# Dilated attention moved into the middle run's block, and the final output moved into the second run with its first two rows of tokens split early

## The reference, cut to what matters

```
first_block:  h = rms_norm(x)
              a = gelu/silu branch with a spatial mix of tokens
              b = attention over 12 heads in three groups, dilated by 1, 4 and 16,
                  joined by the groups' maxima and sums of exponentials
              m = attention over 256 memory tokens
              x = x + (gates_0 * (a @ proj_a) + gates_1 * (b @ proj_b) + gates_2 * (m @ proj_m)) @ w_out
second_block: h = rms_norm(x) * (1 + scale) + shift
              y = [ssm branch | differential attention, 4 heads | window attention]
              x = x + gate * (y @ w_out_2)
              return rms_norm(x, final_gain)
```

## Time and profile before

| | us |
|---|---|
| median of 3 runs | 1859.37 (1856.37 to 1862.62) |
| the profiled execution, its own time | 1859.85 |
| its span | 1858.1 |
| PE busy | 1764.0 (95%) |
| DVE busy | 914.3 (49%) |
| ACT busy | 654.6 (35%) |
| POOL busy | 248.9 (13%) |

### The profile page before, as it was taken

One profiled execution on the slowest core, in us unless ns is written; L12 is line 12 of the kernel. 1 busy time (PEld: TensorE's weight loads), 2 busy tenths in 40 slices (PEclk: granted clock), 3 DMA queues, 4 the chain that ended last, 5 costly groups with the idle time before them and its releaser, 6 DMA issues. The chain is left out here.

```text
span 1858.1 us, 22280 instructions
## 1 busy us (share of the span) xinstructions
PE 1764.0 (95%) x8828; PEld 1430.4 (77%) x8828; DVE 914.3 (49%) x1504; ACT 654.6 (35%) x1204; POOL 248.9 (13%) x412
## 2 busy tenths in 40 slices
PE   6999989899999899999999999798999999999698
PEld 5788867688887788778888788687887777777587
DVE  5128887545333664573223322366152545656654
ACT  5224337512233333562211211233223453435531
POOL 3002210288601100000000000490000000000000
PEclk9999999899999999999999999899999999999799
DMA  3211100235322210211111111332613101000042
GB/s 137 62 59 45 46 23 2 87 102 181 111 78 94 68 46 24 74 42 39 44 51 54 45 55 29 113 125 95 131 35 94 46 24 35 23 24 35 23 147 102
DMA packets 146577, 123.07 MB, mean 66 GB/s; under 512 B 8859, under 2 KB 132106, under 8 KB 145802
## 3 DMA queue, kind: packets, MB, share of 16 engines
q1 hardware_dynamic: 146474, 121.65, 21.6%
HBM read 108.37 MB, written 13.26 MB: 65 GB/s over the span
## 5 line engine op out<-in xcount | busy, mean ns | idle before, releaser
L81 PE MATMUL psum<-hT,w_parts 128*128 128x512 f32 x3360 | 801.7, 395 | 24.5 <-DVE w_parts L185 13.6
L81 PEld LDWEIGHTS psum<-hT,w_parts 128*128 128x128 f32 x3360 | 634.3, 190 | 163.1 <-DVE w_parts L185 15.8
L185 DVE TENSOR_TENSOR w_parts<-w_raw,w_parts 128x1024 fp32r<-128x1024 f32 x104 | 132.2, 1271 | 482.1 <-ACT w_parts L181 481.8
L81 PE MATMUL psum<-h2T,w_parts 128*128 128x512 f32 x1248 | 301.9, 399 | 5.0 <-PEq L2162 5.0
L81 PEld LDWEIGHTS psum<-h2T,w_parts 128*128 128x128 f32 x1248 | 234.5, 191 | 55.0 <-issue 6.8
L1385 ACT ACTIVATE gate<-psum,cols 128x512 f32<-128x512 f32 x48 | 33.1, 689 | 292.5 <-PE psum L81 292.5
L181 ACT CAST w_parts<-w_raw 128x1024 fp32r<-128x1024 f32 x104 | 108.3, 1041 | 65.5 <-DMA w_raw<-w_in 49.1
L81 PE MATMUL psum<-y_high,wp_parts 128*128 128x512 f32 x384 | 128.7, 395 | 0.3 <-DVE ya_low L1443 0.3
L81 PE MATMUL psum<-w_parts,y_parts 128*128 128x512 f32 x384 | 89.2, 395 | 7.7 <-DVE y_parts L1726 7.7
L81 PEld LDWEIGHTS psum<-w_parts,y_parts 128*128 128x128 f32 x384 | 73.4, 192 | 23.5 <-issue 8.1
L81 PEld LDWEIGHTS psum<-y_high,wp_parts 128*128 128x128 f32 x384 | 72.0, 188 | 18.5 <-DVE ya_low L1443 1.5
(11 more groups left out here) (358 smaller groups left out, 2227.6 us busy)
## 6 DMA issues: line engine op xcount, KB each, us to landing
w_raw<-w_in SPq DMA_DIRECT2D x94, 512.0 KB, 4.0
middle_a<-ada_w SPq DMA_DIRECT2D x32, 384.0 KB, 3.7
w_raw<-w_out SPq DMA_DIRECT2D x16, 512.0 KB, 4.4
qkT<-x SPq DMA_DIRECT2D x8, 512.0 KB, 8.0
w_raw<-m_w_kv SPq DMA_DIRECT2D x8, 512.0 KB, 3.8
base<-x SPq DMA_DIRECT2D x8, 512.0 KB, 4.4
x_kept<-x_ring SPq DMA_DIRECT2D x8, 512.0 KB, 2.6
base<-x_kept SPq DMA_DIRECT2D x8, 512.0 KB, 3.6
```

The costliest lines, as they stand in the source:

```text
L81: last = pe.matmul(out, lhs(a, k), rhs(b, k), start=(k == 0 and n == 0), stop=(k == depth - 1 and n == 2))
L185: dve.tensor_tensor(self.parts[:, u, LO, :, :], self.raw[:, :, :], self.parts[:, u, HI, :, :].bitcast(F32), ALU.subtract).then_inc(self.lo ...
```

## The change

`stage_attention` becomes `DilatedAttention`, an object beside the middle run, with the same instructions in the same order in the methods for the run's start. The clearing of the semaphores moves from behind the dilated attention to ahead of it. Tile 0's high part is made on ACT ahead of the last move, its low part on DVE ahead of the last store, and TensorE may begin slot 0 with it. SP issues tile 1's load before the loads of `Join`, `Modulation` and `SsmMatrices`, and these wait until the last unit is stored.

`stage_output` becomes `FinalOutput`, an object beside the second run. There is no block's end and no clearing between the two. Bodies 31 to 38 are written out among the output's own work. The weights' rows come in the order 0, 1, 2, 3, 6, 7, 4, 5 through three raw buffers; rows 4 and 5 belong to the last two heads of the differential attention. The first 256 tokens of `yT` are split in five pieces by rows: the first piece (rows 0 and 1) within the run, at the slot before the last, into the place of the ring of tokens, and four after it. The other tokens are split by tiles as before.

```diff
     def sync(self, sp):
...
             if n or not w.ahead:
                 w.load_tile(sp, self.tiles[n].view)
-            for work in self.beside:
-                if n == 0:
+            if n == (1 if w.ahead else 0):
+                for work in self.beside:
                     work.sync(sp, -1)
-                elif n == 1:
-                    work.sync_second(sp)
...
+class DilatedAttention(Attention):
+    def sync_start(self, sp):
+        self.w.ahead_load(sp)
+    def sync(self, sp, s):
+        if s == -1:
+            sp.wait_ge(self.stored, self.n)
+    def tensor_start(self, pe):
+        for u in range(self.n + self.lag + 1):
+            super().tensor(pe, u)
+        pe.wait_ge(self.maxed, self.n)
+    def tensor(self, pe, s):
+        if s == 0:
+            pe.wait_ge(self.stored, self.n)
+    def scalar_start(self, act):
+        n, lag = self.n, self.lag
+        for u in range(n + lag):
+            if u == n + lag - 1:
+                self.w.ahead_high(act)
+            if 0 <= u - lag:
+                self.move_act(act, u - lag)
+            if u < n:
+                self.exps(act, u)
+        act.wait_ge(self.stored, n)
+    def vector_start(self, dve):
...
+            if u == n + lag:
+                self.w.ahead_low(dve)
+        dve.wait_ge(self.stored, n)
...
             run_dense(core, run)
-            stage_attention(core, window_units(qkT, v, oT, table, table16, maxima, sums), ident,
...
-        core.clear_semaphores(keep=[w_middle.loaded, w_middle.high, w_middle.low])
+            core.clear_semaphores(keep=[w_middle.loaded, w_middle.high, w_middle.low])
+            dilated = DilatedAttention(core, qkv_stack, window_units(qkT, v, oT, table, table16, maxima, sums), ident,
...
+class FinalOutput(Beside):
+    ORDER = (0, 1, 2, 3, 6, 7, 4, 5)
+    PIECES = (slice(0, 2), slice(2, 4), slice(6, 8), slice(4, 5), slice(5, 6))
...
+    def sync_end(self, sp):
+        diff, last, side = self.diff, TT - 1, (TT - 1) % 2
+        sp.wait_ge(*self.ready)
+        for i in range(KT):
+            self.w.load_row(sp, i)
+        sp.wait_ge(diff.mixed, diff.n)
+        sp.dma_start(self.gate[:, :], self.gate_dram).then_inc(self.gate_loaded, 16)
...
+    def tensor_end(self, pe):
+        diff = self.diff
+        diff.body_pe(pe, 31)
+        pe.wait_ge(diff.maxed, diff.n)
+        pe.wait_ge(self.w.low, 1)
+        pe.wait_ge(self.y_low, 1)
+        for h in range(2):
+            if h:
+                pe.wait_ge(diff.normed, 3)
+            for t in range(2):
+                outs, lhs, c0s, width = self.unit(t)
+                self.w.row(pe, 0, outs[h], lhs, c0s[h], width)
+        diff.body_pe(pe, 32)
+        self.row_of_two(pe, 1, 1)
+        diff.body_pe(pe, 33)
+        self.row_of_two(pe, 2, 2)
+        self.row_of_two(pe, 3, 2)
+        self.row_of_two(pe, 4, 3)
+        self.row_of_two(pe, 5, 3)
+        diff.body_pe(pe, 37)
+        self.row_of_two(pe, 6, 4)
+        self.row_of_two(pe, 7, 5)
...
+    def scalar(self, act, s):
+        if s == len(self.run.slots) - 2:
+            act.wait_ge(*self.rows_ready[0])
+            act.wait_ge(*self.ring_free)
+            self.split_high(act, self.piece(0))
+    def vector(self, dve, s):
+        if s == len(self.run.slots) - 2:
+            self.split_low(dve, self.piece(0), 1)
...
+    def vector_end(self, dve):
...
+        diff.early_dve(dve, 31)
+        w.low_row(dve, 0)
+        diff.late_dve(dve, 31)
+        w.low_row(dve, 1)
+        diff.early_dve(dve, 32)
+        self.split_low(dve, self.piece(1), 2)
+        diff.early_dve(dve, 33)
+        w.low_row(dve, 2)
+        w.low_row(dve, 3)
+        diff.early_dve(dve, 34)
+        diff.late_dve(dve, 34)
+        self.split_low(dve, self.piece(2), 3)
+        diff.late_dve(dve, 36)
+        w.low_row(dve, 4)
+        w.low_row(dve, 5)
```

More of the change, by code:

```diff
@@ L216, in __init__ @@
         self.high = core.sem("w_high")
         self.low = core.sem("w_low")
-    def semaphores(self):
-        return self.loaded + [self.high, self.low]
-    def rows(self):
-        return range(2 if self.early else 0, KT)
-    def load_row(self, sp, k):
-        if k >= 2:
-            sp.wait_ge(self.low, k - 1)
-        sp.dma_start(self.raw[:, k % 2, :], self.weights[:, k, :]).then_inc(self.loaded[k % 2], 16)
-    def high_row(self, act, k):
-        act.wait_ge(self.loaded[k % 2], 16 * (k // 2 + 1))
-        act.copy(self.parts[:, HI, k, :], self.raw[:, k % 2, :]).then_inc(self.high, 1)
@@ L234, in low_row, with load_row @@
-    def low_row(self, dve, k):
-        dve.wait_ge(self.high, k + 1)
-        dve.tensor_tensor(self.parts[:, LO, k, :], self.raw[:, k % 2, :],
-                          self.parts[:, HI, k, :].bitcast(F32), ALU.subtract).then_inc(self.low, 1)
-    def sync_end(self, sp):
-        sp.wait_ge(*self.early)
-        for k in range(2):
-            self.load_row(sp, k)
-    def scalar_end(self, act):
-        for k in range(2):
-            self.high_row(act, k)
-    def vector_end(self, dve):
-        for k in range(2):
-            self.low_row(dve, k)
+    def load_row(self, sp, i):
+        m = i % self.depth
+        if i >= self.depth:
+            sp.wait_ge(self.low, i - self.depth + 1)
+        sp.dma_start(self.raw[:, m, :], self.weights[:, self.order[i], :]).then_inc(self.loaded[m], 16)
@@ new lines, in high_row, with low_row @@
+    def high_row(self, act, i):
+        m = i % self.depth
+        act.wait_ge(self.loaded[m], 16 * (i // self.depth + 1))
+        act.copy(self.parts[:, HI, self.order[i], :], self.raw[:, m, :]).then_inc(self.high, 1)
+    def low_row(self, dve, i):
+        k = self.order[i]
+        dve.wait_ge(self.high, i + 1)
+        dve.tensor_tensor(self.parts[:, LO, k, :], self.raw[:, i % self.depth, :],
+                          self.parts[:, HI, k, :].bitcast(F32), ALU.subtract).then_inc(self.low, 1)
@@ L252, in fetch, with row @@
     def fetch(self, sp):
-        for k in self.rows():
-            self.load_row(sp, k)
+        for i in range(KT):
+            self.load_row(sp, i)
     def split_high(self, act):
-        for k in self.rows():
-            self.high_row(act, k)
+        for i in range(KT):
+            self.high_row(act, i)
     def split_low(self, dve):
-        for k in self.rows():
-            self.low_row(dve, k)
+        for i in range(KT):
+            self.low_row(dve, i)
+    def row(self, pe, i, out, lhs, c0, width):
+        k = self.order[i]
+        for n, (a, b) in enumerate(PASSES):
+            last = pe.matmul(out, lhs(a, k), self.parts[:, b, k, c0:c0 + width], start=(i == 0 and n == 0),
+                             stop=(i == KT - 1 and n == 2))
+        return last
@@ L274, in products @@
                 for out, c0 in zip(outs, c0s):
-                    last = product(pe, out, lhs, lambda part, j: self.parts[:, part, j, c0:c0 + width], [k])
+                    last = self.row(pe, k, out, lhs, c0, width)
                 if made and k == KT - 1:
@@ L2558, in follow @@
                 body += 1
-        self.rest = range(body, self.NORM_AT[3] + 5)
+        assert body == 31
     def at(self, s, half):
@@ L2922, in first_block @@
         w_gates = SplitTiles(core, stack, [(24, lambda n: gate_tile(order[0], 0))], shares=w)
-        middle.prepare(w_middle, maxima, sums, oT, ybT, stat, w_gates)
+        middle.prepare(w_middle, dilated, maxima, sums, oT, ybT, stat, w_gates)
         run_dense(core, middle.run)
@@ L3009, in __init__, with prepare @@
                                wait=lambda h, j=j: self.turn_av.wait(2 * j + h)) for j in range(6)]
-    def prepare(self, w, maxima, sums, oT, ybT, stat, ahead):
+    def prepare(self, w, dilated, maxima, sums, oT, ybT, stat, ahead):
         core, A, later, mergedT, N = self.core, self.A, self.later, self.mergedT, SSM_GROUPS
```

496 lines of the change are left out of this document (254 added, 242 removed).

## The result

| | before | changed |
|---|---|---|
| median, us | 1860.99 (1856.37 to 1863.01, 4 runs) | 1839.67 (1837.20 to 1841.68, 4 runs) |
| ratio of the medians | | 0.9893, 95% interval 0.9874 to 0.9913 |
| profiled execution, its own time | 1859.85 | 1840.56 |
| its span | 1858.1 | 1838.8 |
| PE busy | 1764.0 (95%) | 1759.5 (96%) |

The changed kernel is 21.3 us faster by the medians and 19.3 by the profiled executions; the forecast was 18.9 less, 1840.5, in a range of 1836.5 to 1846. Timed once more beside other kernels it had 1836.69 us, ratio 0.9887 (0.9870 to 0.9903).

A forecast was written before the change was run, and what follows sets the result against it. TensorE, busy nearly all the span, bounds the kernel. The first place (middle run's start) gives 4.5 us, the second (second run's end and output) 14.4: 18.9 less than 1859.85 is 1840.95, 1840.5 for the median; range 1836.5 to 1846.

The forecast's parts named there:

- Border with clearing: Ahead of the dilated attention: clearing moved there makes the attention start 0.8 to 1.4 us later, taken as 1.2.
- Tile 0: Start of the middle run: TensorE begins slot 0 at about 348.3, its idle time falling from 5.03 to about 1.3 us.
- The join: Middle run's start: `join_sel` lands at 357.5, so DVE begins the masks at 357.6 instead of 362.10, 4.5 us less.
- The bound without the toll: At the join: gain of 5.6 us if the 512 KB loaded ahead of `join_sel` delay it not at all.
- First piece: Near the second run's end: DVE waits for ACT at the first piece of `yT`, making the chain 1.3 us late.
- Up to row 1: Tail: unit 31's transpose at 1749.6, rows 0 and 1 among the attention's last steps, row 2 beginning at 1753.5.
- Rows 2 to 7: Output's first tiles: 0.7 us wait at row 4; third tile begins at 1771.9 against 1786.3, 14.4 us less.
- The clock in the tail: Rival: TensorE's clock falls to half in the tail all the same, giving 1842 to 1844.5 us; chance 0.17.
- DVE is no bound: Rival judged: DVE bounds the tail, TensorE waiting 3 to 4 us in all at rows 4 to 7, 1844; chance 0.08.
- The join's loads: Rival: `join_sel` lands at 361 whatever is ahead of it, the join giving 1 us, 1844 in all; chance 0.06.
- The weights' rows: Rival: rows 3 to 7 take 8.8 us to land, third tile at 1778, 1847 in all; chance 0.05.
- Gaps not filled: Rival: row 0 and the pieces fill no gap in the tail but the border goes, 1845.5 us; chance 0.02.

The follow-up runs named there:

- e2: The kernel before with the output's change alone, the dilated attention staying a block of its own: 1843.04 us against 1860.24, ratio 0.9910.
- e3: The changed kernel with SP issuing the loads of join, modulation and SSM matrices ahead of tile 1's load, as before the change: 1846.51 us, ratio to before 0.9930.
- e5: The changed kernel with the first piece's low part on DVE one slot later: 1836.09 us, ratio to before 0.9880.
- e4: The changed kernel with rows 0 and 1 of the output behind the attention's last products on TensorE, not between its bodies: 1842.52 us, ratio to before 0.9906.
- e6: The changed kernel with each of the weights' rows 3 to 7 loaded twice, SP waiting for the first load to land: 1847.64 us, ratio to before 0.9945.
- e0: The changed kernel itself, unaltered, timed again beside other kernels: 1836.69 us, ratio to before 0.9887.
- e7: The changed kernel with DVE's masks waiting for the load of `places` alone, `join_sel` having its own semaphore: 1836.25 us, ratio to before 0.9878.
- e8: The changed kernel with the changes of e7 and e5, and on DVE the attention's own steps ahead of the weights' rows: 1833.59 us, ratio to before 0.9866.

## Why the prediction was right

The time lay in the range and within 1 us of the forecast, and most steps can be read off. Point by point:

- **Border with clearing, 0.8 to 1.4, taken as 1.2.** TensorE's idle time ahead of the dilated attention went from 5.73 us to 7.1, that is 1.4: the upper end. The rest of the 2.09 by which the attention starts later is the first run: the attention starts between 276.5 and 278.5 in the ten traces with the clearing ahead of it, at 275.2 and 275.5 in the two without.
- **Tile 0.** Slot 0 was put at 348.3 with an idle time of 1.3: 348.42 and 1.25. The start agrees in part by luck: the attention began 2.09 us later, not 1.2, and was 0.67 us shorter.
- **The join, 4.5.** Masks were put at 357.6 and came at 356.27, 5.8 us earlier than before and 4.8 earlier than in e2, which has the old order too. The mechanism is shown by e3. The mis-sized term is the landing of `join_sel`: 7.0 us plus a toll of 1.1 for the 512 KB ahead of it, and it landed after 6.9. The twelve traces show which part was off. Without those 512 KB ahead of it, it took 7.0 (before), 6.2 (e2) and 6.2 us (e3); with them 6.5 to 7.3 in nine traces, 6.9 in the median. `places` took 5.2 to 5.4 us without and 5.8 to 6.6 with them. So there is a toll, of some 0.7 us by the medians, and the 7.0 that the sum started from was the highest of the three. The bound without the toll, 5.6, comes near the measured 5.8 because the landing of 7.0 that it uses is too long by about as much as the toll that it leaves out, not because there is no toll. The Trainium skill's rule (DMA: Bandwidth & Descriptors, Queues, rings and completion order) says that a semaphore's increment lands only after every earlier write of that DMA engine, and was read as speaking for the lower gain. Tile 1 had landed by 352.52, when ACT began its cast, so its last byte held up nothing at 356, and the rule has no bearing on the toll that is left.
- **What the join left out.** The prediction counted the masks' start alone. Measured from the last products, and so without the border, the join went from 25.34 to 18.16 us, 7.2 less, or 4.8 less than in e2. The low clock in the matmuls on the masks costs 1.7 us (4.47 for 2.81). It is there in all seven traces of the changed order and in one of the two of the old. The prediction named a low clock as a sign there, but no term of the sum had it.
- **First piece.** DVE waited 3.71 us (3 to 4 were said), unit 28's transpose came 1.4 us late after 1.29 of waiting (1.3). e5 takes it away and has 1.2 back.
- **Up to row 1.** In the time of the profile before (the last slot's first half starts 4.62 us earlier now, 1724.94 for 1729.56) unit 31's transpose is at 1749.45, forecast 1749.6, and row 2 at 1753.07, forecast 1753.5. TensorE's wait ahead of that transpose is 1.30 us, where 1.5 to 2 were said.
- **Rows 2 to 7.** The wait at row 4 is 0.57 (0.7). The last matmul ends at 1832.25; 65.2 us ahead of that is 1767.05, or 1771.67 in the old time, against 1771.9 in the sum. The second place gave 14.7 us, 14.4 were said.
- **The root behind its table load.** In the changed kernel the load begins at 1725.41 and takes 1.28, the root begins at 1726.71, 0.02 behind it. The drain of 1.4 us that the Trainium skill (ScalarE: Activation LUTs, What ACT_TABLE_LOAD costs) adds would have put DVE's wait at 5.1; it was 3.71.

**The rivals.** The clock in the tail didn't fall; e4 shows that it does, for 1.6 us of cost in the first 24 matmuls, if the gaps aren't filled. DVE is no bound, with 0.57 us of waiting at row 4. The join's loads did come earlier. The weights' rows landed in 3.6 us in the median, 4.5 at most, and not 8.8. "Gaps not filled" was priced at 5 us above the forecast (4.7 by its own terms, 14.4 less 7.7 and 2), and e4's tail is 4.9 longer. The point from which the change would lose was put at 15 us of landing; nothing ran near it, and e6 doesn't test it. Two more of the signs were missed: `join_sel` landed 6.9 us after its issue and not 8, and TensorE went on at 356.68, 7.9 us after the end of the last store (348.81) and not some 12; by the prediction's own schedule, with the join's loads issued behind that store at 349 and the masks at 357.6, it would have been some 9.

That 18.9 and the 19.29 of the profiled executions agree so well is partly luck. Net of its later start the first place gave 5.8 us instead of 4.5 by the next dense slot (364.04 for 369.80), the tail 14.7 instead of 14.4, and the middle gave 1.1 back, which no step had foreseen. The profiled execution of e0, the same program with a middle of 1356.4 us, took 1835.17, which is below the range of 1836.5 to 1846; the median of that comparison, 1836.69, is only just within it.

## What to carry to other kernels

Ask of a moved DMA which instruction waits for it on the next engine and what is queued behind that: at the join 6.6 us hung on one load's place in the queue. A wait for two transfers should be split when the first user needs only one of them. Fill the gaps in the chain that is last with work that is ready anyway, chain first and filler second, and cut the timeline at marks on the busiest engine, since the time of a whole execution hides a gain of 2 or 3 us that each piece shows to a few tenths.

## What the runs showed of the hardware

- The same work (the middle) took 1356.4 to 1360.9 us in twelve traces; in the stretch from 520 to 800 us two traces of one program had a mean granted clock of 0.97 and 0.98. The middle's spread is 4.5 us; the changed kernel's eight executions, 1835.17 to 1841.68 us, spread by 6.5.
- A load of 256 KB landed 6.2, 6.2 and 7.0 us after its issue with 774 KB issued ahead of it, and 6.5 to 7.3 us with 1.3 MB issued in the 1.0 us ahead. The load of 512 KB at the head of that queue was there after some 4.2 us.
- After a wait of 2.47 us in the join the granted clock was 0.57 in the next stretches, near its lower level; after one of 0.95 us in e7 it stayed at 1.00. In nine traces with the changed join the 24 matmuls behind the wait took 4.35 to 4.47 us where it was 2.14 to 2.87 us (seven traces), and 2.81 where it was 0.95 (e7) and 1.66 (e8). In e2, where slot 0 had begun at the lower level, they took 2.81 behind 2.38.
- A load of the table for the root took 1.28 us, and the root began 0.02 us behind it.
